# Small fp32 products of two mixers in another order: halves side by side in the recurrence, full-array products first in the state space outputs

## The reference

```python
def wkv7(r, w, k, v, a, b):                  # 4 heads of 64
    def step(state, inp):
        r_t, w_t, k_t, v_t, a_t, b_t = inp
        sa = einsum('bhij,bhj->bhi', state, a_t)
        state = state * w_t + sa * b_t + v_t * k_t
        return state, einsum('bhij,bhj->bhi', state, r_t)
    ...
def s5_mixer(u, ...):                        # 16 groups, 64 complex states each
    ...
    _, _, x_re, x_im = lax.associative_scan(_complex_affine_combine, (ar, ai, bu_re, bu_im), axis=1)
    y = einsum('gcn,bsgn->bsgc', c_re, x_re) - einsum('gcn,bsgn->bsgc', c_im, x_im)
    y = y.reshape(bsz, seq, D_MIX) + d * u32
    h = gelu(y) @ glu_w
```

## Time and profile before

| | us |
|---|---|
| median of 3 runs | 2429.18 |
| lowest, highest | 2426.09, 2433.64 |
| the profiled execution | 2424.82 |
| its span | 2423.0 |

### The profile page before, as it was taken

The page is one execution under the profiler, slowest core; times in us unless marked ns, Lnnn a source line. Parts: engine busy times, 40 slices in busy tenths (PEclk is TensorE's granted clock), DMA queues, the critical chain, the costliest instruction groups (busy, mean ns, idle before and its releaser), DMA issues.

```text
span 2423.0 us, 26808 instructions
## 1 busy us (share of the span) xinstructions
PE 2202.3 (91%) x10424; PEld 1738.7 (72%) x10424; DVE 1302.9 (54%) x1822; ACT 465.4 (19%) x897; POOL 858.7 (35%) x1016
## 2 busy tenths in 40 slices
PE   5889888998799999999789999998997689999995
PEld 5667677776678888878547878787776358788784
DVE  6772745335672343655454745546553746727274
ACT  2111400120110000300462201112202642102021
POOL 3322323222344444444103444444432014444441
PEclk8997999998899999999889999999998889999998
DMA  7865667456889999988207889898876028889895
GB/s 253 232 140 113 139 117 156 102 134 157 265 206 197 196 192 192 192 178 185 63 1 171 189 182 196 174 193 187 188 159 134 1 62 188 186 189 193 180 194 122
DMA packets 121349, 393.55 MB, mean 162 GB/s; under 512 B 25172, under 2 KB 27348, under 8 KB 120712
## 3 DMA queue, kind: packets, MB, share of 16 engines
q0 software_dynamic: 96624, 350.46, 67.8%
q1 hardware_dynamic: 24600, 41.39, 5.3%
HBM read 387.92 MB, written 3.92 MB: 162 GB/s over the span
## 4 chain that ended last, share of the span: by engine, by line
PE 76%; DVE 13%; DMA 5%; ACT 2%; issue 2%; POOL 0%; SPq 0%; DVEq 0%; ACTq 0%
PE ps L1474 64%; DMA w_lo<-in_w 3%; PE ps L1581 2%; PE ps L1562 2%; PE ps L1597 2%; DMA w_hi<-in_w 1%; DVE small L800 1%; PE ps L1516 1%; DVE work L625 1%; PE ps L1732 1%; DMA arena<-in_ada 1%; ACT arena L1414 1%; DVE arena L827 1%; ACT arena L1422 1%; PE ps L1676 1%
## 5 line engine op out<-in xcount | busy, mean ns | idle before, releaser
L1474 PE MATMUL ps<-h_hi,w_hi 128*128 128x512 f32 x1760 | 706.6, 401 | 27.6 <-DVE h_lo L469 14.9
L1474 PE MATMUL ps<-h_lo,w_hi 128*128 128x512 f32 x1760 | 689.7, 392 | 0.0
L1474 PE MATMUL ps<-h_hi,w_lo 128*128 128x512 f32 x1760 | 689.1, 392 | 0.0
L381 POOL DMA_DIRECT2D w_hi<-in_w x334 | 185.4, 555 | 1368.1 <-PE ps L1474 1355.5
L1474 PEld LDWEIGHTS ps<-h_hi,w_hi 128*128 128x128 f32 x1760 | 332.8, 189 | 117.1 <-issue 20.4
L1474 PE MATMUL ps<-g_hi,w_hi 128*128 128x512 f32 (+1 forms) x880 | 346.5, 394 | 42.5 <-DVE g_lo L423 24.8
L1474 PEld LDWEIGHTS ps<-h_hi,w_lo 128*128 128x128 f32 x1760 | 333.0, 189 | 70.9
L1474 PEld LDWEIGHTS ps<-h_lo,w_hi 128*128 128x128 f32 x1760 | 333.4, 189 | 69.9 <-issue 4.4
L386 POOL TENSOR_SCALAR w_lo<-w_hi 128x1024 fp32r<-128x1024 f32 x334 | 361.0, 1081 | 43.0 <-DMA w_hi<-in_w 37.3
L1474 PE MATMUL ps<-g_lo,w_hi 128*128 128x512 f32 (+1 forms) x880 | 340.8, 387 | 0.0
L1474 PE MATMUL ps<-g_hi,w_lo 128*128 128x512 f32 (+1 forms) x880 | 340.6, 387 | 0.0
(11 more groups left out here) (375 smaller groups left out, 2047.4 us busy)
## 6 DMA issues: line engine op xcount, KB each, us to landing
w_hi<-in_w POOLq DMA_DIRECT2D x334, 512.0 KB, 3.9
w_lo<-in_w POOLq DMA_DIRECT2D x334, 512.0 KB, 5.6
arena<-in_ada SPq DMA_DIRECT2D x40, 512.0 KB, 6.7
x<-in_ada SPq DMA_DIRECT2D x8, 512.0 KB, 6.5
x<-in_xT SPq DMA_DIRECT2D x1, 2048.0 KB, 10.1
x<-in_xT SPq DMA_DIRECT2D x4, 512.0 KB, 4.9
arena<-in_memT SPq DMA_DIRECT2D x2, 1024.0 KB, 5.2
out_y<-arena SPq DMA_DIRECT2D x1, 2048.0 KB, 6.3
```

What stands on the lines that cost most here:

```text
L381: pool.dma_start(w_hi[:, q % SLOTS, :], A["w"][q]).then_inc(S(f"high_in{q % SLOTS}"), 16)
L1474: mm = pe.matmul(bank, w[:, slot, cols], a(k), start=(k == 0 and i == 0), stop=(k == blocks - 1 and i == 2))
```

## The change

In the state space outputs the 16 products of `toep` are issued first, ahead of the wait for the states. Then the products of the states follow with g as the innermost loop. Since the products of one bank no longer follow each other, each bank is begun once (start at s == 0) and ended once.

In the recurrence each operation is issued for both halves before the next one. The wait for the state at the head of a step is for both halves at once, and the operations of the output are put in another order, the one with 128 rows last.

```diff
             pe.wait_ge(S("s5_toep"), 1)
+            for s in range(S5T):
+                for g in range(2):
+                    pe.matmul(ps[6 + g][:, NQ * s:NQ * s + NQ], m["toep"][:, 2 * s + g].rearrange("p j c -> p (j c)"), m["u_turned"][:, 2 * s + g, :],
+                              start=(s == 0), stop=False, skip_group_check=True)
             need("s5_states")
             for s in range(S5T):
-                for g in range(2):
-                    cols = slice(NQ * s, NQ * s + NQ)
-                    pe.matmul(ps[6 + g][:, cols], m["toep"][:, 2 * s + g].rearrange("p j c -> p (j c)"), m["u_turned"][:, 2 * s + g, :],
-                              start=True, stop=False)
-                    for part in range(2):
+                for part in range(2):
+                    for g in range(2):
                         mm = pe.matmul(ps[6 + g][:, NQ * s + 1:NQ * s + NQ], m["g"][halves[g], part, s, :],
-                                       m["w"][halves[g], part, NQ * s:NQ * s + NQ - 1], start=False, stop=(part == 1))
+                                       m["w"][halves[g], part, NQ * s:NQ * s + NQ - 1], start=False,
+                                       stop=(part == 1 and s == S5T - 1), skip_group_check=True)
...
                 now = c % 2
+                need("state_set", 2 if c else 1)
                 for p in range(2):
-                    need("state_set", 1 if c or p == 0 else 0)
                     pe.matmul(ps[4 + p][rows[p], 0:HD], bd["akT"][rows[p], c, :], bd["vt"][rows[p], c, :], start=True, stop=False)
+                for p in range(2):
                     pe.matmul(ps[4 + p][rows[p], 0:HD], pad("a")(p, c), state[:, now, p, :], start=False, stop=True).then_inc(S("rec_y"), 1)
...
                 for p in range(2):
                     pe.matmul(ps[4 + p][:, at_s], bd["kt"][rows[p], c, :], bd["vt"][rows[p], c, :], start=True, stop=False)
+                for p in range(2):
                     need("rec_sa_copied1" if p else "rec_sa_copied")
                     pe.matmul(ps[4 + p][:, at_s], rw_bt[rows[p], c, :], chain_y[rows[p], 1, :], start=False, stop=True).then_inc(S("rec_state"), 1)
                 for p in range(2):
-                    pe.matmul(ps[6 + p][rows[p], at_o], pad("r")(p, c), state[:, now, p, :], start=True, stop=False)
-                    pe.matmul(ps[6 + p][rows[p], at_o], bd["rbT"][rows[p], c, :], chain_y[rows[p], 1, :], start=False, stop=False)
-                    mm = pe.matmul(ps[6 + p][rows[p], at_o], bd["rkT"][rows[p], c, :], bd["vt"][rows[p], c, :], start=False, stop=True)
+                    pe.matmul(ps[6 + p][rows[p], at_o], bd["rbT"][rows[p], c, :], chain_y[rows[p], 1, :], start=True, stop=False)
+                for p in range(2):
+                    pe.matmul(ps[6 + p][rows[p], at_o], bd["rkT"][rows[p], c, :], bd["vt"][rows[p], c, :], start=False, stop=False)
+                for p in range(2):
+                    mm = pe.matmul(ps[6 + p][rows[p], at_o], pad("r")(p, c), state[:, now, p, :], start=False, stop=True)
                 mm.then_inc(S("rec_o"), 1)
```

## The result

| | before | after |
|---|---|---|
| median us | 2431.2 (4 runs) | 2388.39 (4 runs) |
| lowest, highest | 2426.09, 2433.64 | 2378.88, 2395.3 |
| profiled execution, its span | 2424.82, 2423.0 | 2383.48, 2381.7 |

The ratio is 0.9828, 95% interval 0.9802 to 0.9853: 42.8 us less by the medians, 41.3 by the profiled executions. A second measurement of the changed kernel (after_again) gave 0.9849 (0.9829 to 0.987), 36.2 us by the medians. The forecast was 2394.0, in a range of 2386 to 2406, so 35.2 us saved.

A forecast was written before the change was run, and what follows sets the result against it. The prediction took TensorE's own instruction stream as the bound. Savings of 18.0 us in the recurrence and 17.2 us in the state space products sum to 35.2, from the median 2429.18 to 2394.0 us, range 2386 to 2406.

The forecast's parts named there:

- TensorE's stream is the bound at both places, and nothing takes the time back: State space outputs and recurrence: TensorE's own instructions are what is late, and later stretches stay as long; 35.2 us saved.
- rival 4: Later stages: clock, weights or the outputs' DMA round trip give back half of one part, about 9 us, 2403; chance 0.08.
- Recurrence, 18.0 us: Recurrence: head saves 0.50 us a step, output products 0.62, state products nothing; 1.12 us over 16 steps, period about 6.80.
- The added wait costs nothing; slack 1.5 us: Head of a recurrence step: waiting for both state halves is free unless DVE is over 1.5 us late.
- Rival 5: Recurrence head, L1779: the joined state wait makes a chain of latencies, slower, 2437 or more; chance 0.02.
- Column pairs: Recurrence: halves using all 128 rows and differing in columns only pack, a pair costing one half plus 0.01 us.
- Rival 1: Recurrence, new L1781 and L1800: column pairs do not pack, 8.3 us less saved, 2402; chance 0.06.
- Rival 6: Both places: halves written apart already run side by side; for the recurrence only, 2412; chance 0.03.
- State space outputs, 17.2 us: State space block: first products fill the 2.31 us idle, state products pair at half clock; end at 199.2 instead of 216.46.
- Rival 2: State space block: the clock stays full, L1676 ends at 195.7; 40.1 us saved, 2389; chance 0.12.
- The sum: Whole kernel: 18.0 us from the recurrence plus 17.2 from the state space products, 35.2 us saved.

The follow-up runs named there:

- rec_only: The kernel before with the new order of the recurrence alone: 2412.86 us, ratio 0.9921.
- rec_half_by_half: The changed kernel with each half whole before the other in the recurrence's state and output products, the 128-row product still apart behind them: 2385.63 us.
- split_wait: The changed kernel with the wait for the state at the head of a recurrence step apart again for each half: 2383.25 us in one execution.
- s5_wait_first: The kernel before with only the state space outputs reordered, but the wait for the states again ahead of all products: 2412.99 us in one execution.
- s5_half_then_half: The kernel before with only the state space outputs reordered, but all 32 state passes of one half ahead of the other's: 2416.85 us, one execution.
- s5_one_bank: The kernel before with only the state space outputs reordered, but the two state products of one half next to each other: 2402.12 us, one execution.

## Why the prediction was right, and where it was off

- *TensorE's stream is the bound at both places, and nothing takes the time back.* Right: 37.8 us at product 1351, and still 37.8 at 3601. The 1.4 to 2.4 us that many traces lose between the two places are far from the 9 of rival 4, which is out. The prediction didn't mention the wait for DMA at the first head; it cost nothing, because the chain behind that transfer moved forward with TensorE.
- *Recurrence, 18.0 us.* Right: 18.4 in after, 17.3 in rec_only. The head was priced at 0.52 and measured 0.52, the outputs 0.64 and 0.64, the period 6.80 and 6.78. The new order of the state products was priced at nothing, and rec_half_by_half shows nothing.
- *The added wait costs nothing; slack 1.5 us.* Right on both: 1.5 us of slack, and split_wait's step is no shorter. Rival 5 is out.
- *Column pairs.* L1781 and L1800 pack, as L1664 did: four passes in 0.26 us. Rival 1 is out. The rule of the Trainium skill ("TensorE: Matmul & The Clock Gate", Part 3, Packing small matmuls) that a weight load overlaps a product in flight only when the row group differs did not keep these pairs apart, though all of them use the same 128 rows.
- *Rival 6, that halves written apart run side by side already*, is out for the kernel before: 18 us came. It holds once the shapes stand together (rec_half_by_half).
- *State space outputs, 17.2 us.* The mechanism was right and this term was too small: 21.8. The step that failed is "the new block is sparse from the same moment, so I take half clock for L1676". It carried over a clock from a stretch whose cause the change removed. Rival 2 happened, with its 0.12: L1676's successor took 3.7 us, not 6.8, and the half-speed start of the projection went too. Both of its reasons are borne out: with the idle time left in (s5_wait_first), or with the pairs taken out (s5_half_then_half), the clock falls. A small misreading beside it: the prediction has the clock full again some four microseconds after dense products resumed; in the trace of before it is half from 216.5 to 219.5 us and full from there, so three.
- *The sum.* 35.2 forecast; with the clock of rival 2, 40.1; the places in the trace give 40.2 (21.8 and 18.4). The measured 42.8 and the 36.2 of the second measurement lie on either side. That the 36.2 comes so near to the forecast 35.2 is luck: the term of the state space outputs was 4.6 us too small, and the spread of the executions hid it.

## What to carry to other kernels

Group small products by the shape of array they use, before thinking of pairs: each change of shape costs a group of its own and keeps the halves apart, while halves within a few places of each other find one another. Put work that waits for nothing ahead of a wait even where it is short, since an idle TensorE followed by small products can leave those products at half clock: 2.3 us of idle time cost 10. And when a change removes the idle time in front of a stretch, don't price the stretch at the clock that it had.

## What was unexpected of the hardware

- Products of the two row halves do not start strictly in the order of the queue. In rec_half_by_half all four passes of L1795 start ahead of those of L1796 (446.73 and 446.90), though half 1's L1795 stands behind half 0's L1796 in the queue. In s5_one_bank the order within the line can't be read from the rows, but 64 passes in 3.8 us leave no room for a half that waits for its turn. The Trainium skill ("TensorE: Matmul & The Clock Gate", Part 3, Packing small matmuls) says that products keep the order of the program in start and end; the rows of L1795 and L1796 differ from it.
- The overlap of the halves reaches only a few places: 27 passes in 2.90 us without a partner in s5_half_then_half, against 64 passes in 3.8 us in s5_one_bank. How far it reaches was not measured.
- The clock can fall with no idle time at all: to half at 200 us in s5_half_then_half (0.51 is the mean from 200 to 207).
- The same attention stretch of the same program took 167 us in one execution and 172 in another, with granted clocks of 0.87 and 0.85. A saving of 3 us can't be read from the total of single executions.
